# Cross attention, first three heads: products with the values 256 queries wide, from high and low parts

## The reference

```python
def cross_attn(h, mk, mv, w_q, w_o):
    bn, L, _ = h.shape
    q = (h @ w_q).reshape(bn, L, CA_HEADS, CA_HEAD_DIM)
    o, _ = attend(q, mk, mv, jnp.ones((L, mk.shape[1]), dtype=bool))
    return o.reshape(bn, L, -1) @ w_o
```

## Time and profile before

| | us |
|---|---|
| median of 3 runs | 2787.7 (2787.18 to 2787.85) |
| profiled execution, its own time | 2788.41 |
| its span, first to last instruction | 2786.4 |
| TensorE busy | 2765.0 (99%) |
| VectorE busy | 1719.2 (62%) |
| POOL busy | 1450.8 (52%) |
| ScalarE busy | 897.5 (32%) |

### The profile page before, as it was taken

The page is one execution under the profiler, slowest core; times in us unless marked ns, Lnnn a source line. Parts: engine busy times, 40 slices in busy tenths (PEclk is TensorE's granted clock), DMA queues, the critical chain, the costliest instruction groups (busy, mean ns, idle before and its releaser), DMA issues. The chain is left out here.

```text
span 2786.4 us, 61044 instructions
## 1 busy us (share of the span) xinstructions
PE 2765.0 (99%) x22847; PEld 2659.1 (95%) x22847; DVE 1719.2 (62%) x3178; ACT 897.5 (32%) x2009; POOL 1450.8 (52%) x1178
## 2 busy tenths in 40 slices
PE   9999999999999999999999999999999999999998
PEld 8888999999999999999998889999999999999998
DVE  5555743247866766887963346432478667668877
ACT  4333412232422222443413344222324222224434
POOL 2222343433577777787532112433335777777776
PEclk9999999999999999999999999999999999999999
DMA  4100124331232322633123331243312222326332
GB/s 140 38 30 30 61 91 159 121 122 39 77 117 80 121 106 97 215 130 130 54 91 110 113 109 60 88 163 121 116 45 77 106 91 110 116 89 223 129 130 77
DMA packets 85189, 286.95 MB, mean 103 GB/s; under 512 B 11230, under 2 KB 21470, under 8 KB 76056
## 3 DMA queue, kind: packets, MB, share of 16 engines
q10 hardware_dynamic: 46973, 152.08, 15.5%
q1 hardware_dynamic: 38051, 132.55, 14.0%
HBM read 225.26 MB, written 59.59 MB: 102 GB/s over the span
## 5 line engine op out<-in xcount | busy, mean ns | idle before, releaser
L682 POOL TENSOR_SCALAR w_hi<-w_raw 128x512 fp32r<-128x512 f32 x236 | 153.7, 669 | 954.0 <-PE linear L831 751.3
L686 POOL TENSOR_TENSOR w_lo<-w_raw,w_hi 128x512 fp32r<-128x512 f32 x420 | 590.0, 1416 | 100.8 <-ACT w_hi L1667 84.5
L831 PE MATMUL linear<-h_hi,w_hi 128*128 128x344 f32 x1134 | 372.8, 329 | 2.4 <-issue 1.7
L831 PE MATMUL linear<-h_lo,w_hi 128*128 128x344 f32 x1134 | 362.2, 319 | 0.0
L831 PE MATMUL linear<-h_hi,w_lo 128*128 128x344 f32 x1134 | 362.2, 319 | 0.0
L686 POOL TENSOR_TENSOR w_lo<-w_sum,w_hi 128x512 fp32r<-128x512 f32 x186 | 270.0, 1452 | 145.0 <-ACT w_hi L1667 144.2
L1221 PE MATMUL ps_scores<-c,w_hi 128*128 128x258 f32 x1512 | 288.6, 283 | 0.0
L1221 PE MATMUL linear<-c,w_hi 128*128 128x258 f32 x1344 | 247.3, 284 | 1.1 <-POOL w_lo L686 1.1
L831 PE MATMUL linear<-g_hi,w_hi 128*128 128x344 f32 x744 | 240.3, 323 | 0.0
L831 PE MATMUL linear<-g_hi,w_lo 128*128 128x344 f32 x744 | 237.7, 319 | 0.0
L831 PE MATMUL linear<-g_lo,w_hi 128*128 128x344 f32 x744 | 237.4, 319 | 0.0
(11 more groups left out here) (483 smaller groups left out, 7210.9 us busy)
## 6 DMA issues: line engine op xcount, KB each, us to landing
w_raw<-in_w SPq DMA_DIRECT2D x214, 512.0 KB, 3.7
hid_spill<-hid_out ACTq DMA_DIRECT2D x22, 1032.0 KB, 4.4
t_spill<-hid_joined ACTq DMA_DIRECT2D x20, 1032.0 KB, 3.9
y_val<-t_spill ACTq DMA_DIRECT2D x40, 516.0 KB, 4.0
kv_slotc<-in_mem_cache_k ACTq DMA_DIRECT2D x8, 2048.0 KB, 8.4
kv_slotc<-in_mem_cache_v ACTq DMA_DIRECT2D x8, 2048.0 KB, 9.7
w_more<-in_w SPq DMA_DIRECT2D x32, 512.0 KB, 5.5
y_val<-hid_spill ACTq DMA_DIRECT2D x30, 516.0 KB, 5.0
```

What stands on the lines that cost most here:

```text
L682: pool.tensor_scalar(out, src, 1.0, 0.0, ALU.mult, ALU.add).then_inc(sem["hi_split"], 1)
L686: return pool.tensor_tensor(out, src, hi.bitcast(F32), ALU.subtract).then_inc(sem[event], 1)
L831: mm = pe.matmul(out, w[:, slot, cols], a, start=(k == 0 and j == 0), stop=(k == n - 1 and j == 2))
```

## The change

In heads 0 to 2 of each layer, six head phases in all, the products with the values are made for two jobs at once, 256 queries wide, and from reduced parts. The values' transposes (`turn_value`, two and two, in the bank `v_bank`) and the jobs' transposes (`turn_job`, in two PSUM banks in turn) are each copied by ScalarE to a high part (`value_high`, `job_high`) and subtracted by VectorE to a low part (`value_low`, `job_low`). `mix_pair(k)` then multiplies for jobs 2k and 2k+1: twelve matmuls, three terms for each half of the columns and of the memory. `pair_out` copies 512 columns at once. The transposed parts of a pair have one buffer, `pt_pair`, in chunk 7 of `mixc`; the low values lie in chunk 6, the high ones where `vnatc` is. The order of all three engines is written out anew, and TensorE's has two key parts, the sample's products and the last pair in another order than before. The last head keeps the code of before (moved behind the new branch), and so do the sample's own products, in `mix_sample`.

```diff
-            out.append((f"cross{l}_{h}", 1, 6 if h < CA_HEADS - 1 else 5,
-                        job_events(len(JOBS["mem"]) + 1) | {"q_spread": 1, "v_turned": 1, "v_ready": 1}))
+            jobs, wide = len(JOBS["mem"]), h < CA_HEADS - 1
+            out.append((f"cross{l}_{h}", 1, 6 if wide else 5,
+                        job_events(jobs + 1) | {"q_spread": 1, "v_turned": 1, "v_ready": 1} | (
+                            {"v_turned": 2, "v_ready": 2, "v_low": 2, "turned_low": jobs, "mixed": jobs // 2 + 1,
+                             "mixed_out": jobs // 2 + 1} if wide else {})))
         out.append((f"casplit{l}", 1, 0, {"hi_ready": 12, "lo_ready": 12}))
...
+        pt_pair = over(("pt_pair", [P, 2, 2, 2 * P], F32R), start=places["mixc"] + 4 * 7 * TOK)[0]
+        v_high = over(("v_high", [P, 2, MEM], F32R), start=places["vnatc"])[0]
+        v_low = over(("v_low", [P, 2, MEM], F32R), start=places["mixc"] + 4 * 6 * TOK + 2048)[0]
...
+        v_bank = ps_s[:, 512:1024].rearrange("p (m d) -> p m d", m=2)
+        def turned_bank(job):
+            return ps_t[:, 512 * (job % 2):512 * (job % 2) + MEM].rearrange("p (m n) -> p m n", m=2)
...
+                    def turn_value(c):
+                        pe.wait_ge(sem["freed_dve"], at("freed_dve", ph, 0, 8 + c))
+                        if c == 0:
+                            pe.wait_ge(sem["mixed_out"], at("mixed_out", ph))
+                        else:
+                            pe.wait_ge(sem["v_low"], at("v_low", ph, 0, 1))
+                        for m in range(2):
+                            mm = pe.transpose(v_bank[:, m, P * c:P * c + P], vc[h][:, c, P * m:P * m + P], ident[:])
+                        mm.then_inc(sem["v_turned"], 1)
+                    def turn_job(job):
+                        pe.wait_ge(sem["normed"], at("normed", ph, 0, order_s("mem", job) + 1))
+                        if job == "sample":
+                            for m in range(2):
+                                mm = pe.transpose(v_bank[:, 0, P * m:P * m + P], psc[:, P * m:P * m + P], ident[:])
+                        else:
+                            if job >= 2:
+                                pe.wait_ge(sem["turned_low"], at("turned_low", ph, 0, job - 1))
+                            for m in range(2):
+                                mm = pe.transpose(turned_bank(job)[:, m, :], p_c[job % 2][:, P * m:P * m + P], ident[:])
+                        mm.then_inc(sem["turned"], 1)
+                    def mix_pair(k):
+                        if k == 0:
+                            pe.wait_ge(sem["v_low"], at("v_low", ph, 0, 2))
+                        if k == 3:
+                            pe.wait_ge(sem["drawn"], at("drawn", ph, 0, 1))
+                        else:
+                            pe.wait_ge(sem["mixed_out"], at("mixed_out", ph, 0, k))
+                        pe.wait_ge(sem["turned_low"], at("turned_low", ph, 0, 2 * k + 2))
+                        terms = ((v_high, 0), (v_high, 1), (v_low, 0))
+                        for c in range(2):
+                            for m in range(2):
+                                for j, (v, part) in enumerate(terms):
+                                    mm = pe.matmul(ps_o[:, 2 * P * c:2 * P * c + 2 * P], v[:, m, P * c:P * c + P], pt_pair[:, part, m, :],
+                                                   start=(m == 0 and j == 0), stop=(m == 1 and j == 2))
+                        mm.then_inc(sem["mixed"], 1)
...
+                    def mix_sample():
+                        pe.wait_ge(sem["turned_in"], at("turned_in", ph, 0, 7))
+                        pe.wait_ge(sem["mixed_out"], at("mixed_out", ph, 0, 3))
+                        pe.wait_ge(loads["v_slot"], slot_value(l, 1, h))
+                        past_waits()
...
+                    if h < CA_HEADS - 1:
+                        pe.wait_ge(sem["freed_dve"], at("freed_dve", ph, 0, 7))
+                        step("S", "sample")
+                        step("S", 0)
+                        turn_value(0)
+                        p = unit(ph, 0, 4, p, [(0, MEM)], mem_hi, mem_lo, slot=slot)
+                        step("S", 1)
+                        turn_value(1)
+                        step("S", 2)
+                        turn_job(0)
+                        step("S", 3)
+                        turn_job(1)
+                        step("S", 4)
+                        turn_job(2)
+                        step("S", 5)
+                        turn_job(3)
+                        mix_pair(0)
+                        step("S", 6)
+                        turn_job(4)
+                        step("S", 7)
+                        turn_job(5)
+                        mix_pair(1)
+                        key_part(0)
+                        turn_job(6)
+                        turn_job("sample")
+                        key_part(1)
+                        mix_pair(2)
+                        turn_job(7)
+                        key_part(2)
+                        mix_sample()
+                        key_part(3)
+                        mix_pair(3)
+                        last = step
+                        continue
...
+                    def exponential(job):
+                        n = order_s("mem", job)
+                        o = n % 2
+                        act.wait_ge(sem["biased"], at("biased", ph, 0, n + 1))
+                        if job != "sample" and job >= 2:
+                            act.wait_ge(sem["turned"], at("turned", ph, 0, job - 1))
+                        act.activation(psc[:, :] if job == "sample" else p_c[job % 2], score_banks["mem"][o][0][:, 0:MEM], ACT.Exp,
+                                       scale=1.0 / 16.0, bias=bias[:, 2 * o:2 * o + 1], accum_out=den[:, 2 * o:2 * o + 1]
+                                       ).then_inc(sem["exped"], 1)
+                    def value_high(c):
+                        act.wait_ge(sem["v_turned"], at("v_turned", ph, 0, c + 1))
+                        copy(v_high[:, :, P * c:P * c + P], v_bank[:, :, P * c:P * c + P]).then_inc(sem["v_ready"], 1)
+                    def job_high(job):
+                        act.wait_ge(sem["turned"], at("turned", ph, 0, job + (2 if job == 7 else 1)))
+                        act.wait_ge(sem["mixed"], at("mixed", ph, 0, job // 2))
+                        past_waits()
+                        half = P * (job % 2)
+                        copy(pt_pair[:, 0, :, half:half + P], turned_bank(job)).then_inc(sem["turned_in"], 1)
+                    def pair_out(k):
+                        act.wait_ge(sem["mixed"], at("mixed", ph, 0, k + (2 if k == 3 else 1)))
+                        past_waits()
+                        copy(mixc[:, 2 * h:2 * h + 2, 2 * P * k:2 * P * k + 2 * P], ps_o[:, :].rearrange("p (c n) -> p c n", c=2)
+                             ).then_inc(sem["mixed_out"], 1)
+                    if h < CA_HEADS - 1:
+                        exponential("sample")
+                        act.dma_start(kv_slotc[:, :], dram["mem_cache_v"][l, h]).then_inc(loads["v_slot"], 16)
+                        exponential(0)
+                        value_high(0)
+                        exponential(1)
+                        value_high(1)
+                        act.wait_ge(sem["freed_dve"], at("freed_dve", ph, 0, 9))
+                        act.dma_start(dram["mem_v"][l, h].rearrange("p c n -> p (c n)"), mixc[:, 2 * h + 1, 512:1024]
+                                      ).then_inc(stored["v"], 16)
+                        exponential(2)
+                        job_high(0)
+                        exponential(3)
+                        job_high(1)
+                        exponential(4)
+                        exponential(5)
+                        job_high(2)
+                        pair_out(0)
+                        job_high(3)
+                        exponential(6)
+                        exponential(7)
+                        job_high(4)
+                        pair_out(1)
+                        job_high(5)
+                        act.wait_ge(sem["turned"], at("turned", ph, 0, 8))
+                        copy(ptc[:, 0:MEM], ps_s[:, 512:512 + MEM]).then_inc(sem["turned_in"], 1)
+                        job_high(6)
+                        act.wait_ge(stored["v"], stored_before(l, 1, h + 1))
+                        pair_out(2)
+                        job_high(7)
+                        act.wait_ge(sem["mixed"], at("mixed", ph, 0, 4))
+                        copy(drawnc[h][:, 0:512], ps_o[:, :]).then_inc(sem["drawn"], 1)
+                        pair_out(3)
+                        continue
...
+                    def value_low(c):
+                        dve.wait_ge(sem["v_ready"], at("v_ready", ph, 0, c + 1))
+                        part = slice(P * c, P * c + P)
+                        dve.tensor_tensor(v_low[:, :, part], v_bank[:, :, part], v_high[:, :, part].bitcast(F32), ALU.subtract
```

(61 more changed lines are left out.)

19 lines of the change are left out of this document (2 added, 17 removed).

## The result

The median went from 2787.85 us (2786.00 to 2792.07, 21 runs) to 2793.62 us (2790.55 to 2797.68, 21 runs). The ratio is 1.0017, 95% interval 1.0011 to 1.0022: the change costs 4.7 us (3.1 to 6.1). Predicted were 2794.0 us and a range of 2785 to 2802.

What follows compares the result with a forecast made beforehand. TensorE, busy throughout six 26.9 us stretches, was taken as the bound. Per head -1.52 (instructions) - 0.7 (old waits) + 3.3 (new waits) = +1.05 us, six +6.3: 2787.7 + 6.3 = 2794.0 us, range 2785 to 2802.

Steps and rivals of the forecast that it cites:

- TensorE's instructions: Per head, eight value steps (7.28 us) give way to four pairs of 1.44 us (5.76 us): 1.52 us saved.
- The waits: TensorE waits eight times in a new stretch, 3.3 us a head; 0.7 us of old waits go.
- the walk: Three queues stepped through in code order from the sample scores' first load; stretch 27.9 us, chance 0.6 with waits 2.8 to 4.0.
- The subtraction: VectorE's low part, 128x256 out of PSUM: 0.42 us, pitch 0.34 us, 0.47 us until TensorE starts.
- the half case: Half of the four waits for low parts vanish: waits 1.9 us a head, 2786 us; chance 0.1.
- edge of 0.2%: 5.6 us, about what a measurement can tell from no change; faster 0.1, within 0.35, slower 0.55.
- That the low parts are not late: VectorE overlaps enough that four waits at transposes, 2.2 of 3.3 us, vanish: 2781.1 us; chance 0.1.
- The cover: Next head's query weights, cast by POOL from the first key part on, are ready in time: costed at nothing.
- The POOL case: Normalise 7 waits for POOL's cast, up to 0.83 us, delaying all behind: 11.3 us slower, 2799 us; chance 0.18.
- The clock: TensorE's clock falls from 2.4 to 1.2 GHz in the changed stretches: at most 148 us, 2936 us; chance 0.02.

Runs made afterwards that it cites:

- e4: Changed kernel with the same operations, the order of all three engines' queues rewritten in heads 0 to 2; 2778.97 us, ratio 0.9965 to the kernel before.
- e7: e4 with the eight subtractions of the probabilities left out of each head, same products issued; 2780.60 us.
- e6: Changed kernel with e4's new order on ScalarE and VectorE alone, TensorE keeping its order; 2802.49 us.
- e5: Changed kernel with e4's new order on TensorE alone, ScalarE and VectorE keeping theirs; 2824.29 us.
- e1: Changed kernel with a second pt_pair buffer for odd pairs in heads 0 and 1, head 2 keeping one; 2787.95 us.
- e2: Changed kernel with the eight subtractions of the probabilities left out of each of the six heads, same products issued; 2786.35 us.
- e9: e4 with e1's second pt_pair buffer in heads 0 and 1; 2779.83 us.

## Why the prediction came out right, and where its size was off

**TensorE's instructions: right.** A pair took 1.43 us for the predicted 1.44. e4 bears out the other end of the sum: 26.9 us less 2.2 is 24.7, and e4 takes 24.98 with the few tenths of waits that it has left (0.24 us ahead of scores 3, 0.17 ahead of the sample's products).

**The waits: the right places, 2.8 us instead of 3.3.** This is the mis-sized term. The stretch is 27.4 us; without the 24.6 us that the walk has for instructions, 2.8 are left, the lower bound of the walk; so a head lost 0.5 us, not 1.05, and six lost 3.3 us, not 6.3. The gaps in brackets ahead of scores 3, transposes 1, 2, 3, 4, 6 and the sample's products add up to more, 3.5 us, but those between scores and transposes (1 to 4) count some 0.2 us each more than they cost: where TensorE isn't late, loads go from scores to transposes in 0.76 us (429.02 to 429.78), matmuls in 0.87 us, and late transposes pass on sooner, as told below. Up to pair 0 the walk is within 0.12 us: from the first load at 413.41, transposes 2 came at 11.25 us (predicted 11.23), pair 0 at 12.67 (12.79). Two prices were too high. A step of transposes that TensorE was late for passes on after 0.17 us (428.85 to 429.02), not 0.22; with five such steps that is 0.25 us. And the sample's copy starts 2.0 us after the first load (436.72 to the copy at 438.74), not 2.2, so pair 3 waits 0.1 us and not 0.29. Together that is 0.45 of the 0.47 us by which the walk's 27.88 was too long. The sample's copy:

```profile
438.74 0.60 ACT L1772 ACTIVATE mixc<-linear 128x512 f32<-128x512 f32 x1 [1.82 <-PE linear L1161]
```

**The subtraction: right.** 0.42 us, and its links as priced. One of its two sources was misread: line 2941 of the earlier trace rows adds and multiplies, it doesn't subtract, but it is as long. Two slips in the sums change little: -1.52 - 0.7 + 3.3 is 1.08, not 1.05, and the half case leaves 3.3 - 1.1 = 2.2 us of waits, not 1.9, which is 2787.7 us and not 2786.

**The total is better than its working, by luck.** 2794.0 against 2793.62 agrees because some 2 us came on top that the prediction doesn't have; the measured 3.3 us added to its 2787.7 would give 2791.0. The profile shows 3.3 us in the stretches; between the two medians lie 5.8 us, by the ratio 4.7. Outside the stretches the span grew by 0.5 us. Over all kernels here the time from the first load of layer 0's output projection to the first stretch of layer 1 went from 1207.4 to 1211.3 us, 1208.5 before and 1209.3 after, with the same code in it. The interval's lower end, 3.1 us, would leave nothing to explain. Whether the rest is such scatter or an effect on the feed-forward part wasn't settled. By the prediction's edge of 0.2% the ratio of 1.0017 is within, to which it gave 0.35, and not slower, to which it gave 0.55; the interval reaches over the edge.

**The rivals.** That the low parts are not late, and the half of that, were wrong: all of the predicted gaps are there. What spoke against them, a chain of steps and not a lack of time, is what e4 and e7 show. The cover held: the next query unit's first load comes 0.12 us behind the last of pair 3 (440.71 to 440.83). The POOL case missed by little: normalise 7 runs from 431.64 to 431.99 and POOL's cast starts at 432.12.

```profile
431.64 0.35 DVE L2810 TENSOR_SCALAR pc_ring<-pc_ring,inv 128x256 f32<-128x256 f32 x1
```

```profile
432.12 1.20 POOL L694 TENSOR_SCALAR w_hi<-w_raw 128x512 fp32r<-128x512 f32 x2 [11.38 <-PE linear L1102]
```

That its mechanism and price are real is seen in e6, 1.33 us against the 1.18 of the earlier trace rows. The Trainium skill's page "SBUF — State Buffer", section "SBUF: two separate sides", calls the ports that VectorE's two-port operations share with POOL an exclusive lock, which one holds for a whole instruction while the other is fully blocked. The trace agrees: the normalise, in SBUF, was held up, the subtraction out of PSUM beside POOL's cast in e6 (433.76, two in 0.75 us) was not. The clock stayed at 1.00 in the changed stretches.

**What the prediction didn't see.** It weighed the change as written. The work was 2.2 us a head cheaper, and 1.9 of that was to be had (26.90 to 24.98 us in e4): the waits were the order's.

## What to carry to other kernels

Where engines walk hand-written queues and one of them is full, an edit is priced by two sums: what the full engine's instructions save, and what each later hand-over makes it wait in this very order. When the second eats the first, write the queues of all engines anew together before dropping the edit; here one half alone lost 4 us (e6) or at least 6 us (e5) a head against the whole. A buffer or an operation that looks costly (e1, e2) may cost only through its place: try it again in the better order (e9, e7).

## What the hardware showed unasked

TensorE's granted clock fell in e5 after its longest idle times. In head 0 its loads stood still for 1.82, 0.65 and 2.68 us:

```profile
430.43 0.20 PEld L1131 LDWEIGHTS ps_turned<-ident,pc_ring 128*128 128x128 f32 x2 [1.82 <-DVE pc_ring L2809]
431.28 0.30 PEld L1147 LDWEIGHTS linear<-pt_pair,v_high 128*128 128x128 f32 x2 [0.65 <-issue]
...
437.06 0.21 PEld L1131 LDWEIGHTS ps_turned<-ident,pc_ring 128*128 128x128 f32 x2 [2.68 <-DVE pc_ring L2809]
```

Then, by the windows:

```profile
431.50:437.10 5.60, 3.29 (x25) 2.87 (x24) 1.86 (x8) 1.64 (x6) 0.00 (x0) 1.00 0.00 0
437.10:440.30 3.20, 3.20 (x16) 3.20 (x17) 0.42 (x1) 0.39 (x1) 0.00 (x0) 0.51 0.02 5
440.30:445.80 5.50, 5.39 (x60) 4.41 (x60) 1.27 (x3) 1.86 (x4) 0.00 (x0) 0.97 0.00 0
```

The clock was 0.51 for 3.2 us, the 1.2 GHz level, and pair 2 took some 2.6 us for 1.43; then it came back. In the changed kernel, whose longest gap is 1.17 us, no stretch shows less than 1.00. The same three gaps stand in the head at 1888.46, whose clock stayed at 1.00, and in the first of layer 1, where it fell twice, from 1843.2 on behind the first two gaps and again at the end of the third, from 1850.3 on. So the gaps alone don't decide it. A reorder that makes TensorE wait long can pay twice: 1.3 us in four of the six heads here, 2.8 us in one, nothing in one.

VectorE's normalise in SBUF took 1.07 us beside POOL's low parts (from 426.15 on) in e4 as well, where the key unit stands earlier; it cost nothing, as TensorE had other work in front of it:

```profile
426.55 1.07 DVE L2809 TENSOR_SCALAR pc_ring<-pc_ring,inv 128x256 f32<-128x256 f32 x1
```
